# A half-filled last tile per expert as one stationary operand of high and low parts, and groups of three full tiles and a half

## What is computed

```python
top_val, top_idx = lax.top_k(hf @ w_router + b_router, 4)      # weights = softmax(top_val)
xs = hf[tok]                                                   # rows sorted by expert, 8192 in all
gate, up = jnp.split(lax.ragged_dot(xs, w_gu, group_sizes) + b_gu[sorted_e], 2, axis=-1)
act = (clip(up, -7, 7) + 1.0) * (gate7 * sigmoid(1.702 * gate7))   # gate7 = min(gate, 7)
out = lax.ragged_dot(act, w_down, group_sizes) + b_down[sorted_e]
y = zeros.at[tok].add(out * weights)
```

## Time and profile before

| what | us |
|---|---|
| median of three runs | 4102.62 |
| lowest and highest run | 4099.51 and 4103.07 |
| span of the profiled execution | 4097.7 |

### The profile page before, as it was taken

One profiled execution on the slowest core, in us unless ns is written; L12 is line 12 of the kernel. 1 busy time (PEld: TensorE's weight loads), 2 busy tenths in 40 slices (PEclk: granted clock), 3 DMA queues, 4 the chain that ended last, 5 costly groups with the idle time before them and its releaser, 6 DMA issues. The chain is left out here.

```text
span 4097.7 us, 64304 instructions
## 1 busy us (share of the span) xinstructions
PE 3893.5 (95%) x18356; PEld 3198.7 (78%) x18357; DVE 2347.9 (57%) x3725; ACT 1531.9 (37%) x2258; POOL 570.1 (14%) x600
## 2 busy tenths in 40 slices
PE   7999999898979999999999999999999999999993
PEld 4888788787867878878877788878888788888782
DVE  5263342796775664564675666586555656544752
ACT  3232321572223442333453444364343434322532
POOL 1110110111220111111110201111110211111102
PEclk9999999899989999999999999999999999999997
DMA  6442441764345784565685777597575857544836
GB/s 236 162 134 87 151 144 61 244 213 154 128 148 181 237 285 116 153 233 138 196 280 174 221 243 226 153 344 224 167 233 169 257 170 228 152 135 114 265 102 189
DMA packets 347524, 763.09 MB, mean 186 GB/s; under 512 B 29849, under 2 KB 29906, under 8 KB 342818
## 3 DMA queue, kind: packets, MB, share of 16 engines
q1 hardware_dynamic: 289138, 600.04, 42.8%
q0 software_dynamic: 55120, 151.68, 15.1%
q10 hardware_dynamic: 3200, 10.53, 0.6%
HBM read 653.81 MB, written 108.33 MB: 186 GB/s over the span
## 5 line engine op out<-in xcount | busy, mean ns | idle before, releaser
L1860 ACT CAST weights_split<-weights_raw 128x1024 fp32r<-128x1024 f32 x420 | 432.0, 1055 | 493.9 <-PE tok_bank_acc L118 448.6
L116 PE MATMUL tok_bank_acc<-weights_first,weights_split 128*128 128x512 f32 x1264 | 505.9, 400 | 10.7 <-DVE weights_first L1953 8.4
L1953 DVE TENSOR_TENSOR weights_split<-weights_raw,weights_split 128x1024 fp32r<-128x1024 f32 x420 | 490.5, 1219 | 24.0 <-ACT weights_split L1860 15.7
L116 PE MATMUL tok_bank_acc<-weights_split 128*128 128x512 f32 x1264 | 494.8, 391 | 3.1 <-DVE weights_split L1953 2.8
L1953 DVE TENSOR_TENSOR weights_first<-weights_raw,weights_first 128x1024 fp32r<-128x1024 f32 x416 | 483.7, 1219 | 22.6 <-ACT weights_first L1860 20.2
L1838 POOL DMA_INDIRECT y_rows<-tok_act_row,tok_token x123 | 202.9, 1649 | 2107.9 <-DVE tok_act_row L2022 2058.6
L118 PE MATMUL tok_bank_acc<-weights_first,weights_split 128*128 128x512 f32 x1264 | 494.0, 391 | 0.0
L117 PE MATMUL tok_bank_acc<-weights_first,weights_split 128*128 128x512 f32 x1264 | 493.6, 390 | 0.0
L118 PE MATMUL tok_bank_acc<-weights_split 128*128 128x512 f32 x1264 | 492.1, 389 | 0.0
L117 PE MATMUL tok_bank_acc<-weights_split 128*128 128x512 f32 x1264 | 492.0, 389 | 0.0
L1860 ACT CAST weights_first<-weights_raw 128x1024 fp32r<-128x1024 f32 x416 | 425.5, 1050 | 170.6 <-PE tok_bank_acc L118 122.9
(11 more groups left out here) (327 smaller groups left out, 6739.5 us busy)
## 6 DMA issues: line engine op xcount, KB each, us to landing
weights_raw<-in_w_gu SPq DMA_DIRECT2D x560, 512.0 KB
weights_raw<-in_w_down SPq DMA_DIRECT2D x280, 512.0 KB
tok_bias<-in_b_gu SPq DMA_DIRECT2D x35, 1024.0 KB
early_w_raw<-in_w_in POOLq DMA_DIRECT2D x14, 2048.0 KB, 11.1
proj<-pro_stage SPq DMA_DIRECT2D x112, 256.0 KB, 2.0
pro_w_ada<-in_w_ada POOLq DMA_DIRECT2D x64, 256.0 KB, 3.5
mix_late<-proj SPq DMA_DIRECT2D x48, 256.0 KB, 3.7
mod_w_ada<-in_w_ada SPq DMA_DIRECT2D x8, 1024.0 KB, 14.9
```

The costliest lines, as they stand in the source:

```text
L116: nc.tensor.matmul(out, act_hi, w_hi, start=first, stop=False)
L1860: nc.scalar.copy(whi[c % 2][:, j * SK:(j + 1) * SK], raw[:, n % RAW]).then_inc(hi_done, 1)
L1953: nc.vector.tensor_tensor(wlo[c % 2][:, rows], raw[:, n % RAW], whi[c % 2][:, rows], ALU.subtract).then_inc(lo_done, 1)
```

## The change

An expert's last tile is a half tile if it holds 1 to 64 rows and is not the expert's only one (expert 0 has none by construction). Its rows are gathered, and its operands cut, to 64. Its high and low parts then stand side by side in one stationary operand: columns 0 to 63 high, 64 to 127 low. One step of its product is two matmuls instead of three, by the high and by the low weights. The upper 64 result partitions (the low part's products) are added to the lower 64 by DVE in a new step `join`: an instruction that brings the upper half of the bank, with the bias if there is one, to `half_lo`, and then an add. A group is now up to three full tiles and a half; the half tile has slot 3 (`HALF`) and is the last of its group. The rows of the next group's half tile are transposed in chunk 5 of the group before (`next_half`). The table gets a seventh field, and more steps of DVE and PE make it. POOL copies tokens and shares of full tiles and the half tile separately. The rule of a last single tile is kept, with three in place of four. For the row counts above this gives 71 full and 8 half tiles in 39 groups: ten of one full tile, six of one and a half (experts 1, 15, 16, 21, 27, 29), thirteen of two, one of two and a half, eight of three, one of three and a half. Experts 4, 7 and 12, one group of four tiles before, become two groups of two; expert 28 goes from 4 and 4 to 3, 2, and 2 and a half.

```diff
-GT = 4
+GT = 3
+HALF, HR = GT, P // 2
+SLOTS = GT + 1
-FIELDS = 6
+FIELDS = 7
...
-        fin(nc.vector.tensor_reduce(groups[:], over[:].rearrange("p e (g t) -> p e g t", t=GT)[:, :, :, 0], AX_X, ALU.add))
-
-        for count in (tiles, groups):
-            fin(nc.vector.tensor_scalar(count[:, 0:1], count[:, 0:1], 1.0, None, ALU.max))
+        fin(nc.vector.tensor_scalar(run[:, 0:1], run[:, 0:1], float(HR), None, ALU.add))
+        fin(nc.vector.tensor_scalar(tiles[:, 0:1], tiles[:, 0:1], 1.0, None, ALU.max))
+        over_from("full_from")
+        fin(nc.vector.tensor_scalar(over[:, :, 0], run[:], 0.0, None, ALU.is_gt))
+        fin(nc.vector.tensor_reduce(full[:], over[:], AX_X, ALU.add))
+        fin(nc.vector.tensor_reduce(groups[:], over[:, :, 0:NT:GT], AX_X, ALU.add))
+        fin(nc.vector.tensor_tensor(halves[:], tiles[:], full[:], ALU.subtract))
...
-        for c, src in ((2, cumg), (3, tiles), (4, cumt)):
+        for out, src in ((col[:, 2:3], cumg), (col[:, 3:4], full), (col[:, 4:5], cumt), (half[:, 0:1], halves),
+                         (table[:, 6:7], cumh)):
...
+        nc.tensor.matmul(sm[:, 2 * E:3 * E], hT[:], const("before")[0:E, 0:E], start=True, stop=True).then_inc(table_t, 1)
...
+                with act.If(G.nH > 0):
+                    rows_hi(G.before + G.U + 1, HALF)
...
+        def join(G, c):
+
+            dve.wait_ge(mm_done, G.chunk_tile(c, HALF))
+            lo = acc[HR:P, bank(c, HALF)]
+            if c < NGU:
+                ins = nc.vector.tensor_tensor(half_lo[:], lo, bias[HR:P, column(c):column(c) + N], ALU.add)
+            else:
+                ins = nc.vector.tensor_copy(half_lo[:], lo)
+            ins.then_inc(half_step, 1)
+            dve.wait_ge(half_step, G.halves * 8 + (c + 1 if c < NGU else 2 * c - 3))
...
+                    if t == HALF:
+                        join(G, c)
+                        nc.vector.tensor_tensor(half_lo[:], acc[0:HR, bank(c, t)], half_lo[:], ALU.add).then_inc(half_step, 1)
+                        dve.wait_ge(half_step, G.halves * 8 + 2 * (c - 1))
+                        nc.vector.scalar_tensor_tensor(out=weighted_at(c, t), in0=half_lo[:], scalar=share[0:HR, t:t + 1],
+                                                       in1=g2[0:HR, cols], op0=ALU.mult, op1=ALU.mult).then_inc(read_done, 1)
+                        return
...
+                if c == NGU + 1 and t == 0 and s == 2:
+                    next_half()
...
-                                mm = split_product(nc, acc[:, bank(c, t)], a_hi[:, t, s], a_lo[:, t, s],
-                                                   whi[c % 2][:, s], wlo[c % 2][:, s], s == 0, s == KD - 1)
+                                out, w_hi, w_lo = acc[:, bank(c, t)], whi[c % 2][:, s], wlo[c % 2][:, s]
+                                if t == HALF:
+                                    nc.tensor.matmul(out, a_hi[:, t, s], w_hi, start=(s == 0), stop=False)
+                                    mm = nc.tensor.matmul(out, a_hi[:, t, s], w_lo, start=False, stop=(s == KD - 1))
+                                else:
+                                    mm = split_product(nc, out, a_hi[:, t, s], a_lo[:, t, s], w_hi, w_lo, s == 0,
+                                                       s == KD - 1)
```

More of the change, by code:

```diff
@@ L1234, in routing_programs @@
     tiles, groups, cumg, cumt, sel = (k.sb(n, [P, E]) for n in "tiles groups cumg cumt sel".split())
-    gT, tT = k.sb("gT", [E, P]), k.sb("tT", [E, P])
-    col = k.sb("col", [P, 8])
+    full, halves, cumh = (k.sb(n, [P, E]) for n in "full halves cumh".split())
+    gT, tT, hT = (k.sb(n, [E, P]) for n in ("gT", "tT", "hT"))
+    col, half = k.sb("col", [P, 8]), k.sb("half", [P, 2])
     table = k.sb("table", [P, FIELDS])
@@ L1900, in scalar @@
                     weights_hi(g, n, G.chunks_before(n // PIECES - 1))
-                for t in range(GT):
-                    with act.If(G.T > t):
+                for t in range(SLOTS):
+                    with act.If(G.has(t)):
                         if t < 2:
@@ L1971, in gate_bias @@
             elif t < 2:
-                dve.wait_ge(act_done, G.before * 2 + G.T + 1)
+                dve.wait_ge(act_done, G.before * 2 + G.U + 1)
             else:
@@ L2004, in vector @@
                 G = Group(dve, g)
+                G.halves = field(dve, g, HALVES, E)
                 nT = G.nT
@@ L2039, in vector @@
                         weights_lo(g, PIECES * (c + 1) + n)
-                    if c == 0:
-                        own_rows_lo(3)
-                    for t in range(GT):
-                        with dve.If(G.T > t):
+                    for t in range(SLOTS):
+                        with dve.If(G.has(t)):
                             if c == 2:
@@ L2056, in vector @@
                 weigh(NGU, 0)
-                for t in range(1, GT):
-                    with dve.If(G.T > t):
+                for t in range(1, SLOTS):
+                    with dve.If(G.has(t)):
                         activations_lo(1, t)
                         weigh(NGU, t)
+                with dve.If(G.nH > 0):
+                    rows_lo(G.before + G.U + 1, HALF)
                 with dve.If(nT > 0):
@@ L2111, in tensor @@
                     pe.wait_ge(lo_done, G.pieces(PIECES * c + 1))
-                    for t in range(GT):
-                        with pe.If(G.T > t):
+                    for t in range(SLOTS):
+                        with pe.If(G.has(t)):
                             if c == 0:
-                                pe.wait_ge(xlo_done, G.before * 2 + (2 * t + 4))
+                                pe.wait_ge(xlo_done, G.before * 2 + 6 if t == HALF else G.turn(t) * 2 + 4)
                             if t > 0:
```

246 lines of the change are left out of this document (158 added, 88 removed).

## The result

The changed kernel takes 4032.84 us (median; 4031.81 to 4033.19), the kernel before, run beside it, 4101.07 (4097.26 to 4103.07): a ratio of 0.9836, interval 0.9824 to 0.9848. The forecast was 4039 in a range of 4020 to 4070. The profiled executions last 4031.1 and 4097.7 us, 66.6 apart; the forecast's sum was 63.7.

A forecast was written before the change was run, and what follows sets the result against it. PE's own matmuls were taken as the bound, except in one-tile groups. -87.1 + 14 + 1.2 + 2 + 4.8 + 1.4 = -63.7 us, from a median of 4102.6 to 4039 us; range 4020 to 4070.

The forecast's parts named there:

- Products: PE in the eight half tiles: 16 matmuls a chunk instead of 24, at 0.2268 us each, 87.1 us less.
- does not do what it says: Rival: half-tile matmuls spaced wider or half tiles few; whole gain gone at 0.31 us spacing, 4103 us; chance 0.04.
- Four more groups: Extra groups' weight and bias traffic hidden behind products, costing nothing; chunk 4 waits of up to 0.3 us each, 1.2 us.
- rival with exposed weights: Rival: weights of the four more groups are no longer hidden, 38.7 us each, 4194 us; chance 0.03.
- share of 0.74: DMA's share of its time in two-tile windows before the change, read as showing that added weight traffic stays hidden.
- Chunk 4 of one tile and a half: PE loses 0.5 us at tile 0's transposes and waits 1.8 for the half's low part; six groups, 14 us.
- X: The start of chunk 4 in a group of one tile and a half; PE's and DVE's steps are timed from it.
- no-stall rival: Rival: DVE runs ahead in chunk 4, only table and tail are paid, 4022 us; chance 0.12.
- rival with DVE and DMA as bound: Rival: groups of one and a half lose 8.0 us each, 48 instead of 14, 4073 us; chance 0.13.
- One-tile groups behind a half: Experts 2 and 30 find DVE later and DMAs busier: 1 us each, 2 in all, between 0 and 8 each.
- The table: Longer table steps on DVE and PE, all on the path before the experts: 4.8 us more, bounds 3 and 6.
- The tail: After the last group's last matmul, two more instructions of 0.69 us for its half tile: 1.4 us more.

The follow-up runs named there:

- Run 2: The kernel after, with the low-weights matmul done twice in half tiles, so 24 matmuls a chunk again: 4111.88 us, ratio to before 1.003.
- run 1: The kernel after with no half tile ever formed, 79 full tiles in 40 groups, longer table kept: 4100.23 us, ratio to before 1.0000.
- run 8: The kernel after plus an 8 MB copy within HBM issued with each group's bias load: 4699.55 us in one run, beside 4097.72 of the kernel before.
- Runs 4 to 6: The kernel after, in groups of one tile and a half: DVE's half low part earlier, 4022.06 us; PE's tile 0 transposes earlier, 4028.68; both, 4017.39.
- runs 3 and 7: Two edits of the kernel after: each join's copy of the half's upper rows made twice, 4039.84 us; 2 MB more HBM copy a group, 4057.39 us.
- run 7: The kernel after plus a 2 MB copy within HBM issued behind each group's bias load: 4057.39 us, ratio to before 0.9895.

## Why the prediction was right

**Products.** Predicted -87.1. In a half of the kernel after, PE's matmuls start as before; the first and last of 16, 15 steps of 0.2267 (0.2268 in the earlier trace rows):

```profile
2441.34 0.39 PE L2256 MATMUL tok_bank_acc<-weights_split 128*128 128x512 f32 x1
...
2444.74 0.39 PE L2257 MATMUL tok_bank_acc<-weights_split 128*128 128x512 f32 x1
```

Run 2 gives it back and run 1 shows that the groups and the table without halves gain nothing. The rival "does not do what it says" falls with that.

**Four more groups.** Predicted nothing for traffic and 1.2 for waits; run 1 has the groups alone, five more instead of four, and comes out 2.3 us below before in the expert stretch. The rival with exposed weights, 4194, is refuted. That the share of 0.74 was the reason is not shown: run 8 has a window at 0.79 that grows by 20.8.

**Chunk 4 of one tile and a half.** Predicted 0.5 + 1.8 a group, 14; measured 0.53 + 1.42, 11.7, of which the windows show 10.5. The order was the one laid out; in the second wait PE came 0.2 us later than worked out (X+10.0, with X at 2505.6) and DVE was through 0.2 earlier (2516.54 + 0.41, X+11.4). PE's timeline of one such chunk:

```profile
2508.28 0.60 PE L2184 MATMUL tok_bank_ta<-keep_const,tok_act_row 128*128 128x128 f32 x4
2508.72 1.04 PE L2176 MATMUL tok_bank_tx<-keep_const,tok_rows 128*128 128x128 f32 x8
2510.28 0.50 PE L119 MATMUL tok_bank_acc<-weights_first,tok_a_hi 128*128 128x512 f32 x1 [0.53 <-DVE tok_a_lo L2108]
...
2513.14 0.60 PE L2184 MATMUL tok_bank_ta<-keep_const,tok_act_row 128*128 128x128 f32 x4
...
2517.01 0.50 PE L2256 MATMUL tok_bank_acc<-weights_first,tok_a_hi 128*128 128x512 f32 x1 [1.42 <-DVE tok_a_hi L2108]
```

Runs 4 to 6 take the two waits away, one by one and both. That both come from an order, and not from an amount of work, is shown: the longer one goes when one instruction of DVE moves, the shorter one when PE's transposes move, and no work is removed. The no-stall rival, 4022 us, did not happen by itself; with both waits taken away the time is 4017. The rival with DVE and DMA as bound, 8.0 a group, is refuted by the windows, 1.6 to 1.9 above their tiles, and by runs 3 and 7. DVE is busy for 49.3 us in the window between two such groups, 50 was worked out.

**One-tile groups behind a half.** Predicted 2 for two groups; this term was too small. Their windows are 4.0 and 8.6 above their tiles, before 1.5 and 5.1: +6.1, and +4.3 in the kernel after traced once more. Both are within the 0 to 8 each that the prediction allowed. In the sum it is made up for by terms that came out smaller: the waits (10.5 for 14) and the four more groups (-0.4 in windows that end in larger groups and -1.5 in the other eight one-tile windows, for +1.2). So that the sum came out within 3 us of the spans' difference, 63.7 for 66.6, is in part luck.

**The table.** Predicted 4.8 us. From DVE's first instruction of it to the copy of the word it took 13.08 us before (1209.69 to 1222.77), after 17.71, and in every other kernel with this table 17.7:

```profile
1209.57 0.68 DVE L1533 TENSOR_TENSOR rou_over<-rou_run,keep_const 128x512 f32<-128x512 f32 x1
...
1227.28 0.83 DVE L1995 CAST tok_table<-rou_bank_wt 1x385 int32<-1x385 f32 x1
```

+4.63. PE's first product for the experts starts 4.7 later, the first bias issue 5.0. PE's wait for the table is 7.90 instead of 6.12, and that for the second tile's rows 4.39 instead of 3.98.

**The tail.** Predicted 1.4, measured 1.44: from the start of the last product to that of the last weighing it takes 0.43 us before (4031.78 to 4032.21) and 1.87 after (3964.10 to 3965.97).

**The level.** The forecast added 4.9 us because the span of the profiled execution lay so far under the median of the runs. In all runs recorded here a time is 1.7 to 2.1 us above its own execution's span; the rest of the 4.9 belonged to that one execution, and should not have been carried over. Both kernels' medians here lie nearer to their spans: 4101.07 and 4097.7, 4032.84 and 4031.1. Of the 6 us between 4039 and 4032.84, 2.9 are the sum's (-63.7 for -66.6) and the rest is this.

**What differs from execution to execution.** The table starts at 1205.6 to 1209.7 us in the traces of this study, in kernels that are the same up to there. This goes with the execution and not with a kernel's later code, for it differs as much between two traces of the same kernel: 1209.57 in the kernel after, as above, and in its second trace

```profile
1205.64 0.68 DVE L1533 TENSOR_TENSOR rou_over<-rou_run,keep_const 128x512 f32<-128x512 f32 x1
```

The two traces behind the 66.6 agree in this start to 0.1 us (1209.69 and 1209.57), which is luck. So the spans of single traces of two kernels shouldn't be compared to better than 4 us. In the expert stretch the two traces of the kernel after agree to 0.1 us.

## What to carry to other kernels

Where PE's own matmuls fill the time, an operand of up to 64 rows that comes in a high and a low part can give both parts to one stationary operand: a third of its products goes, at an unchanged price for each. Look then at the first chunk in which a shorter tile asks another engine for something: the price here was two waits of 0.53 and 1.42 us, the longer one for an instruction of 0.4 that stood behind 3 us of work of less haste, and moving it gave 9 us without removing anything. Don't read from a mean share whether a transfer is covered: look for what stands behind the longest burst, the scatters that free a buffer as well as the loads that fill one. And where windows are cut by an instruction of one engine, check what that instruction waited for before you divide the window among the groups.

## What the hardware showed that was not expected

**An idle PE comes back slow.** In run 8 the granted clock is 0.50, the 1.2 GHz level, in the 10 us in which PE does nothing, and 0.57 in the next 10 us, in the last 6.0 of which it works again. In the kernel after the same shows in small: behind a wait of 2.04 us the matmuls of a one-tile group start 0.43 us apart instead of 0.227, at a granted clock of 0.56 from 3818 to 3820 us and of 1.00 in the 3 us before.

```profile
3817.86 0.49 PE L119 MATMUL tok_bank_acc<-weights_first,tok_a_hi 128*128 128x512 f32 x1 [2.04 <-DVE weights_first L2012]
...
3819.41 0.63 PE L120 MATMUL tok_bank_acc<-weights_first,tok_a_hi 128*128 128x512 f32 x1
3819.84 0.63 PE L121 MATMUL tok_bank_acc<-weights_first,tok_a_lo 128*128 128x512 f32 x1
```

So a wait can cost more than its length, and a one-tile window's granted clock is 0.96 in one row of the kernel after and 0.89 in run 7. In the Trainium skill, page "TensorE: Matmul & The Clock Gate", section "Back-to-back issue gap", a matmul takes its columns over 1.2 GHz at the lower level, 427 ns for 512 columns; the trace agrees with 0.42 to 0.43 us.

**Half the partitions, the same time.** DVE's instructions on 64 partitions of 512 elements take 0.68 to 0.69 us, those on 128 the same. The copy of the join, which reads the upper partitions of a bank and writes the lower ones of its tile, has this price too:

```profile
2519.16 0.69 DVE L2030 COPY tok_half_lo<-tok_bank_acc 64x512 f32<-64x512 f32 x1 [2.21 <-PE tok_bank_acc L2257]
```
